# Second mixer: the gate product and the first query product read the input before its norm, and the norm's factor comes in at eviction

## The reference, cut to what matters

```python
x = x + g_f * conv_ffn(...)                # first block: its last product is h @ ffn_w_down
x = rmsnorm(x, final_norm)                 # end of the first block
xn = rmsnorm_2(x, norm_mix_2)              # second block: norm ahead of its mixer
proj = xn @ w_in_2 + b_in_2                # 4608 columns and 16 gate columns
h_q, h_f_fwd, h_f_bwd, h_i, h_g, m_q, ...  = split_cols(proj)
q = silu(h_q)
```

## Time and profile before

| what | value |
|---|---|
| median of 3 runs | 1819.37 us |
| the profiled execution, own time | 1820.89 us |
| its span in the trace | 1819.1 us |
| PE busy | 1725.9 us, 95% |
| DVE busy | 954.3 us, 52% |
| ACT busy | 695.0 us, 38% |
| POOL busy | 148.5 us, 8% |

### The profile page before, as it was taken

One profiled execution on the slowest core, in us unless ns is written; L12 is line 12 of the kernel. 1 busy time (PEld: TensorE's weight loads), 2 busy tenths in 40 slices (PEclk: granted clock), 3 DMA queues, 4 the chain that ended last, 5 costly groups with the idle time before them and its releaser, 6 DMA issues.

```text
span 1819.1 us, 18595 instructions
## 1 busy us (share of the span) xinstructions
PE 1725.9 (95%) x7118; PEld 1276.7 (70%) x7118; DVE 954.3 (52%) x1317; ACT 695.0 (38%) x1016; POOL 148.5 (8%) x158
## 2 busy tenths in 40 slices
PE   7999898989989999999898999989998999999997
PEld 1488644346768888888687877557875778888886
DVE  5867555447444533444639779575534263434343
ACT  2631244311344312333454556874533241313141
POOL 0312200013120000000200000113000100000001
PEclk9999899989999999999899999999998999999999
DMA  9334301330232223222322111334221122233221
GB/s 319 111 115 163 113 10 40 139 116 1 93 91 96 81 74 124 93 75 88 137 103 105 47 47 47 107 122 162 93 93 47 47 93 93 95 110 110 101 92 46
DMA packets 107027, 174.42 MB, mean 96 GB/s; under 512 B 3723, under 2 KB 48267, under 8 KB 106508
## 3 DMA queue, kind: packets, MB, share of 16 engines
q1 hardware_dynamic: 103196, 160.76, 26.0%
q0 software_dynamic: 3760, 12.72, 2.2%
HBM read 169.00 MB, written 4.46 MB: 95 GB/s over the span
## 4 chain that ended last, share of the span: by engine, by line
PE 82%; DVE 7%; ACT 5%; issue 3%; DMA 1%; POOL 1%; SPq 0%; DVEq 0%; ACTq 0%; POOLq 0%
PE bank L822 14%; PE bank L824 14%; PE bank L823 14%; PE bank L855 6%; PE bank L856 6%; PE bank L860 5%; PE bank L876 3%; PE bank L1035 3%; PE bank L1065 2%; PE bank L925 2%; PE bank L1078 1%; PE bank L1005 1%; PE bank L1017 1%; PE bank L1345 1%; PE bank L1376 1%
## 5 line engine op out<-in xcount | busy, mean ns | idle before, releaser
L2916 POOL TENSOR_TENSOR arena<-arena 128x512 f32<-128x512 f32 (+1 forms) x56 | 74.1, 1332 | 986.1 <-ACT arena L1471 982.3
L1440 ACT ACTIVATE weights_hi<-weight_slots 128x2048 fp32r<-128x2048 f32 (+2 forms) x46 | 77.0, 1725 | 123.3 <-DMA weight_slots<-in_ffn_w_down 66.3
L2064 ACT ACTIVATE weights_hi<-weight_slots 128x2048 fp32r<-128x2048 f32 x30 | 55.8, 1908 | 162.0 <-DMA weight_slots<-in_w_up 107.7
L2873 DVE TENSOR_TENSOR weight_slots_lo<-weight_slots,weights_hi 128x2048 fp32r<-128x2048 f32 x30 | 67.4, 2287 | 87.3 <-ACT weights_hi L2064 87.3
L823 PE MATMUL bank<-xn_lo,weights_hi 128*128 128x512 f32 x288 | 112.0, 389 | 0.0
L1426 ACT ACTIVATE arena<-bank 128x512 f32<-128x512 f32 (+3 forms) x110 | 54.7, 537 | 141.9 <-PE bank L824 50.4
L824 PE MATMUL bank<-hx_hi,weight_slots_lo 128*128 128x512 f32 x256 | 99.7, 389 | 0.0
L822 PE MATMUL bank<-sq_hi,weights_hi 128*128 128x512 f32 x256 | 99.6, 389 | 0.0
L823 PE MATMUL bank<-sq_lo,weights_hi 128*128 128x512 f32 x256 | 99.6, 389 | 0.0
L824 PE MATMUL bank<-sq_hi,weight_slots_lo 128*128 128x512 f32 x256 | 99.6, 389 | 0.0
L2114 DVE TENSOR_TENSOR weight_slots_lo<-weight_slots,weights_hi 128x2048 fp32r<-128x2048 f32 (+2 forms) x36 | 70.2, 1990 | 31.1 <-ACT weights_hi L1440 31.1
(11 more groups left out here) (423 smaller groups left out, 4130.5 us busy)
## 6 DMA issues: line engine op xcount, KB each, us to landing
weight_slots<-in_w_in SPq DMA_DIRECT2D x26, 1024.0 KB, 7.1
weight_slots<-in_ffn_w_up SPq DMA_DIRECT2D x22, 1024.0 KB, 7.1
weight_slots<-in_w_mod SPq DMA_DIRECT2D x16, 1024.0 KB, 7.5
weight_slots<-in_w_up SPq DMA_DIRECT2D x16, 1024.0 KB, 6.3
weight_slots<-in_w_down SPq DMA_DIRECT2D x16, 1024.0 KB, 6.2
arena<-in_w_mod POOLq DMA_DIRECT2D x32, 256.0 KB, 3.3
weight_slots<-in_w_out SPq DMA_DIRECT2D x8, 1024.0 KB, 8.5
weight_slots<-in_w_xkv SPq DMA_DIRECT2D x8, 1024.0 KB, 7.5
```

The costliest lines, as they stand in the source:

```text
L1440: A(high_half(kind, n, i), W[:, s_, a:b], ACT.Copy).then_inc(w_hi, 1)
L2064: A(W_hi[:, s % 2, a:b], W[:, s % 2, a:b], ACT.Copy).then_inc(w_hi, 1)
L2873: V.tensor_tensor(W_lo[:, s % 2, a:b], W[:, s % 2, a:b], W_hi[:, s % 2, a:b].bitcast(F32), ALU.subtract).then_inc(w_lo, 1)
L2916: G.tensor_tensor(acc, acc, sq[i % 2][:, 0:width], ALU.add).then_inc(sq_added, 1)
```

## The change

The second mixer's gates and hq are multiplied from xg = x * final_norm * norm_mix_2, without the token factor. ACT writes xg_hi in the loop over the tiles of x, right behind each tile's two squares, by a copy with a scale. DVE writes xg_lo (`gained_low`) inside `half_out`: tile m-1 behind the eviction of product m, for m from 1 on, and tile 7 after the last. DVE then evicts the gates and hq with a multiplication by rstd = r1 * r2, and ACT adds the bias (and takes the silu) in place. PE begins with the high products of tiles 0 and 1, does both norm sums there, and goes on with tiles 2 to 7. hx, normed, is still made for ff, fb and the later slabs. in2 1's high and low parts now stand ahead of hx_hi and hx_lo; x * final_norm * r1 now stands behind the five evictions. in2 1's high parts get a home of their own in the arena, and the product of the gains is formed before the feed-forward stage.

```diff
 PE
-            norm_sum("norm_mid")
-            norm_sum("norm_mix2")
             pe.wait_ge(sem("wgate_lo"), 1)
             w = split_slab("in2", 0)
             ...
             for k in range(KD):
-                pe.wait_ge(x_hi, operand_no["hx", k] + 1)
-                mm(gates[:], wgate_hi[:, k, :], hx_hi[:, k, :], start=k == 0, stop=False)
+                if k == 2:
+                    norm_sum("norm_mid")
+                    norm_sum("norm_mix2")
+                pe.wait_ge(x_hi, operand_no["xg", k] + 1)
+                mm(gates[:], wgate_hi[:, k, :], xg_hi[:, k, :], start=k == 0, stop=False)
 ...
 ACT
                 square_tile("norm_mid", k, x[:, k, :])
                 square_tile("norm_mix2", k, x[:, k, :], scale=pc("final_norm", k))
+                if k == 0:
+                    act.wait_ge(sem("gain_mix2"), 1)
+                A(xg_hi[:, k, :], x[:, k, :], ACT.Copy, scale=gain_mix2[:, k:k + 1]).then_inc(x_hi, 1)
                 if k == KD - 2:
                     split_w("in2", 0)
 ...
+            split_w("in2", 1)
             for k in range(KD):
                 act.wait_ge(normed, norms["norm_mix2"][0] + k + 1)
                 split_x(hx_hi[:, k, :], hx[:, k, :])
-            split_w("in2", 1)
-            ps = full(act, "gates")
-            free(A(zg, ps[:], ACT.Identity, bias=pc("gate_b")), "gates")
+            evicted(act, "gates")
+            A(zg, zg, ACT.Identity, bias=pc("gate_b"))
 ...
 DVE
+            def gained_low(k):
+                dve.wait_ge(x_hi, operand_no["xg", k] + 1)
+                V.scalar_tensor_tensor(xg_lo[k], x[:, k, :], gain_mix2[:, k:k + 1], xg_hi[:, k, :].bitcast(F32),
+                                       ALU.mult, ALU.subtract).then_inc(x_lo, 1)
 ...
                     if half and m == 1:
                         dve.wait_ge(sem("wgate_hi"), 1)
                         V.tensor_tensor(wgate_lo, wgate, wgate_hi.bitcast(F32), ALU.subtract).then_inc(sem("wgate_lo"), 1)
+                    if half and m:
+                        if m == 1:
+                            dve.wait_ge(sem("gain_mix2"), 1)
+                        evicted(dve, f"{kind}_{n - 1}")
+                        gained_low(m - 1)
                     if half and m >= KD - 2:
                         split_w("in2", 0, (m - KD + 2,))
 ...
+            gained_low(KD - 1)
 ...
+            split_w("in2", 1)
             for k in range(KD):
                 split_x("hx", k, hx_lo[:, k, :], hx[:, k, :], hx_hi[:, k, :])
+            for name, dst in [("gates", zg)] + [(f"hq_{m}", q2[:, 512 * m:512 * m + 512]) for m in range(HC)]:
+                ps = full(dve, name)
+                free(V.tensor_tensor(dst, ps[:], rstd[:], ALU.mult), name)
             dve.wait_ge(normed, sum(norms["norm_mix2"]))
             for k in range(KD):
                 V.scalar_tensor_tensor(x[:, k, :], x[:, k, :], pc("final_norm", k), r_mid, ALU.mult, ALU.mult).then_inc(normed, 1)
-            split_w("in2", 1)
```

More of the change, by code:

```diff
@@ L259 @@
 IN2_SPLIT = 6
-HIGH_HOMES = {3: (54, 74), 4: (58, 70), 5: (54, 50)}
+HIGH_HOMES = {1: (32, 40), 3: (54, 74), 4: (58, 70), 5: (54, 50)}
 def split_plan(slab_list):
@@ L271, in operand_plan @@
 def operand_plan():
-    rest = [(n, k) for n in ("hx1", "hc", "mix", "ffn", "hx", "mix2", "mem", "xa", "ao", "mlp") for k in range(KD)]
+    rest = [(n, k) for n in ("hx1", "hc", "mix", "ffn", "xg", "hx", "mix2", "mem", "xa", "ao", "mlp") for k in range(KD)]
     return {k: i for i, k in enumerate(rest)}
@@ L461, in two_blocks @@
         wgate_hi, wgate_lo = (parts("wgate_" + n, a, 2).rearrange("p a c -> p (a c)").rearrange("p (k c) -> p k c", k=KD)
-                              for n, a in (("hi", 42), ("lo", 44)))
+                              for n, a in (("hi", 82), ("lo", 44)))
+        xg_hi = parts("xg_hi", 54, 8)
+        xg_lo = [parts("xg_lo_26", 26, 6)[:, k, :] for k in range(6)] + [parts("xg_lo_14", 14, 2)[:, k, :] for k in range(2)]
         zg, reset = tile(80), tile(81)
@@ L1143, in _ @@
             for k in range(KD):
-                pe.wait_ge(x_hi, operand_no["hx", k] + 1)
-                mm(gates[:], wgate_hi[:, k, :], hx_hi[:, k, :], start=k == 0, stop=False)
-                mm(gates[:], wgate_lo[:, k, :], hx_hi[:, k, :], start=False, stop=False)
+                if k == 2:
[3 more added lines that the diff above has]
+                mm(gates[:], wgate_hi[:, k, :], xg_hi[:, k, :], start=k == 0, stop=False)
+                mm(gates[:], wgate_lo[:, k, :], xg_hi[:, k, :], start=False, stop=False)
                 for c, ps in zip(cols, banks):
-                    mm(ps[:], w[0][:, k, c], hx_hi[:, k, :], start=k == 0, stop=False)
-                    mm(ps[:], w[1][:, k, c], hx_hi[:, k, :], start=False, stop=False)
+                    mm(ps[:], w[0][:, k, c], xg_hi[:, k, :], start=k == 0, stop=False)
+                    mm(ps[:], w[1][:, k, c], xg_hi[:, k, :], start=False, stop=False)
             for k in range(KD):
-                operand("hx", k)
-                ins = mm(gates[:], wgate_hi[:, k, :], hx_lo[:, k, :], start=False, stop=k == KD - 1)
+                operand("xg", k)
+                ins = mm(gates[:], wgate_hi[:, k, :], xg_lo[k], start=False, stop=k == KD - 1)
             end(ins)
@@ L1156, in _ @@
                 for k in range(KD):
-                    ins = mm(ps[:], w[0][:, k, c], hx_lo[:, k, :], start=False, stop=k == KD - 1)
+                    ins = mm(ps[:], w[0][:, k, c], xg_lo[k], start=False, stop=k == KD - 1)
                 end(ins)
             for n, kind in enumerate(["ff", "fb"]):
-                w = split_slab("in2", 1 + n)
+                if n:
+                    w = [(h_, l_) for h_, l_ in zip(*[[v[:, k, :] for k in range(KD)] for v in split_slab("in2", 2)])]
+                else:
+                    pe.wait_ge(w_lo, 2 * split_no["in2", 1] + 2)
+                    lo = low("in2", 1).rearrange("p (k c) -> p k c", k=KD)
+                    w = [(high_parts[1][k // 4][:, k % 4, :], lo[:, k, :]) for k in range(KD)]
                 for m, c in enumerate(cols):
@@ L1163, in _ @@
                     for k in range(KD):
-                        ins = mm3(ps[:], w[0][:, k, c], w[1][:, k, c], hx_hi[:, k, :], hx_lo[:, k, :], k == 0, k == KD - 1)
+                        operand("hx", k)
+                        ins = mm3(ps[:], w[k][0][:, c], w[k][1][:, c], hx_hi[:, k, :], hx_lo[:, k, :], k == 0, k == KD - 1)
                     end(ins)
@@ L1735, in _ @@
                 split_x(hx_hi[:, k, :], hx[:, k, :])
-            split_w("in2", 1)
-            ps = full(act, "gates")
-            free(A(zg, ps[:], ACT.Identity, bias=pc("gate_b")), "gates")
+            evicted(act, "gates")
+            A(zg, zg, ACT.Identity, bias=pc("gate_b"))
             for m in range(HC):
-                ps = full(act, f"hq_{m}")
-                free(A(q2[:, 512 * m:512 * m + 512], ps[:], ACT.Silu, bias=pc("b_in_2", m)), f"hq_{m}")
+                evicted(act, f"hq_{m}")
+                q = q2[:, 512 * m:512 * m + 512]
+                A(q, q, ACT.Silu, bias=pc("b_in_2", m))
             log_exp_tables()
@@ L2405, in _ @@
             link(V.scalar_tensor_tensor(gain_f[:], mod[:, 32:40, 0], 1.0, pc("norm_ffn", 0, 8), ALU.add, ALU.mult))
+            V.tensor_tensor(gain_mix2[:], pc("final_norm", 0, KD), pc("norm_mix_2", 0, KD), ALU.mult).then_inc(sem("gain_mix2"), 1)
             normalise("norm_ffn", lambda k: x[:, k, :], lambda k: gain_f[:, k:k + 1], lambda k: xn[:, k, :])
@@ L2471, in _ @@
                 evicted(dve, f"down_{n}")
-            link(V.tensor_tensor(gain_mix2[:], pc("final_norm", 0, KD), pc("norm_mix_2", 0, KD), ALU.mult))
+            dve.wait_ge(sem("gain_mix2"), 1)
+            gained_low(KD - 1)
             dve.wait_ge(sem("mid_ready"), 1)
```

## The result

| | before | after |
|---|---|---|
| median | 1820.09 us (4 runs, 1817.32 to 1822.19) | 1836.7 us (4 runs, 1835.1 to 1842.17) |
| ratio after to before, 95% interval | | 1.0094 [1.0077, 1.0112] |
| profiled execution, span | 1819.1 us | 1840.4 us (own time 1842.17, the slowest of the four) |
| granted clock, mean | 0.981 | 0.976 |

The change makes the kernel 17 us slower.

A forecast was written before the change was run, and what follows sets the result against it. The prediction took PE's chain as the bound, with time lost where PE waits or runs at half clock. Its terms, 16.1 + 2.6 - 7.7 + 2.6 = +13.6 us, gave a median of 1833.0 us, range 1828 to 1838.

The forecast's parts named there:

- The likeliest case: Whole kernel: all predicted terms come as summed, +13.6 us, median 1833.0 us; chance 54%.
- Term 1: Down products: DVE waits at gained_low(0) for xg_hi 0, holding the cut PE needs for down_12; +16.1 us.
- Term 2: Behind the stall at down_12: PE comes back at half clock; +2.6 us, bounds 1.6 and 3.4.
- Term 3: End of down_15 to ff_0: 34.9 us instead of 42.65, at full clock after a 4.0 us wait; -7.7 us.
- ff_0's cover of hx_lo: Ahead of ff_0: the last hx_lo is ready at 925.3, before ff_0 at 929.4, a cover of 4 us.
- the second rival: Gates' first matmuls and norm sums: the wait for in2 0 drops the clock once more, +2.7 us, 1835.7; chance 18%.
- Term 4: Ahead of fb_0: in2 2's load, issued behind the late store of x, makes PE wait; +2.6 us, bounds 0 and 4.
- The first rival: Ahead of fb_0: in2 2 lands in time or the store is faster, so no wait, 1830.4; chance 20%.
- nothing is added after: Behind the wait at fb_0: ACT and DVE make up their lateness before fb_0 is full; 0 us added.

The follow-up runs named there:

- e1: Changed kernel with the eight xg_lo moved on DVE, behind the evictions of down_13 and down_14 and the cuts of in2 0: 1821.11 us, ratio 1.0014 to before.
- e6: Changed kernel with the high parts of down 5, 6 and 7 taken into ACT's loop over the tiles of x: 1821.38 us, ratio 0.9996 to before.
- e4: Changed kernel with POOL's additions of squares cut to 16 of 512 columns, norm factors no longer the reference's: 1837.49 us, ratio 1.0105 to before.
- e10: Changed kernel with 75 matmuls on idle data ahead of down_12, so PE works through the stall: 1838.65 us, ratio 1.0102 to before.
- e2: Changed kernel with in2 2's load issued ahead of the store of x on SP's queue: 1833.12 us, ratio 1.0073 to before.
- e5: Changed kernel with 68 matmuls on idle data ahead of down_12, the last 2.23 us of the stall left empty: 1838.05 us, ratio 1.0101 to before.
- e9: Changed kernel with e6's and e2's moves, plus in2 0's high parts made and low parts cut earlier: 1808.68 us, ratio 0.9938 to before.
- e11: e9 with 11 matmuls on idle data in the 3.14 us wait ahead of the second projection behind fb_3: 1808.16 us, ratio 0.9934 to before.

## Why the prediction was right, and where its sizes were off

The forecast was 1833.0 us (1828 to 1838) and slower with 0.96; it is 1836.7. The likeliest case came, with more on top of it. That the median stayed inside the range owes something to luck: the terms as the profile has them add up to 21.3 us in place of 13.6, and the profiled execution itself took 1842.17.

- *Term 1, the stall at `gained_low(0)`: predicted +16.1, measured +17.68.* The mechanism is as told: place, releaser, what stands behind it (e1 and e6 take it away by two ways, and the loss goes). xg_lo 0 starts at 860.51, 0.2 us later than predicted. The step that failed is "0.69 us for xg_lo 0, 0.66 us for the eviction and 2.88 us for the two cuts": the cut took 4.37 us, since POOL, set going by the squares at the same moment, adds beside it. 2.88 was read from a stretch in which POOL stood idle. e4 shows it: with POOL's additions cut short 2.91, and a shift of 16.3 us.
- *Term 2, slow clock behind it: predicted +2.6, measured +2.06* in the profile, within the bounds of 1.6 to 3.4. e10 keeps the clock up and gets 1.9 us back there.
- *Term 3, down_15 to ff_0: predicted -7.7, measured -5.61.* The wait ahead of the gates was 3.75 us (4.0 predicted), ff_0's cover of hx_lo held. rstd took 5.5 us (908.37 to 913.83) and not 3.8, which the cover took up. Taking no clock cost was wrong here: the second rival came too, the clock stood at 0.50 until about 904.3, eleven matmuls at 0.43 us. That is 2.5 us by the sum of stretches, against the 2.1 that the term is off. My nearest row, a wait of 3.08 us that left the clock up, was one draw of two: behind that same wait the clock fell in 9 of the 13 profiles and stayed up in 4 (before, after, e2, e5).
- *Term 4, the store ahead of in2 2: predicted +2.6, measured +3.67.* Both were issued at T+6.2 and T+6.6 (T is ff_0's start), the data ended at about T+18.4 (T+17.8 predicted), and the wait is 3.51 us. The first rival (the wait doesn't come) is refuted, and e2 shows that the order on the queue is the cause. Store and load were hardly done faster together than one after the other: from issue to the end of the data the store took 5.5 us alone (902.49 to 908) and the load 7.1 (918.63 to 925.7), both together 12 (938.79 to about 951).
- *Not in the sum: +1.74 between fb_0 and the projection, and +1.8 behind it.* I had set "nothing is added after". The first is the clock, at 0.50 again behind the new wait, by the rows at 960. The second is for the most part the net of the clock's stretches in the rest of the two profiles, 7.5 us lost in after against 6.1 in before: behind the unchanged wait of 3.14 us after lost 3.1 us, before nothing, and before lost more further on.

Of the waits alone (spans less the clock's loss) the difference is 17.7 us. The prediction's own terms without clock are 15.1: 13.6, less 2.6 of term 2, plus the 4.1 us that before lost at its norm sums and gates (1.3 and 2.8 in the sum by stretches), which term 3 had counted as gained. The missing 2.6 us are, to 0.1, what terms 1 and 4 came out larger, 1.6 and 1.1. The profiled run of after is also 5.5 us above its median, so the medians lie 3.7 us above the forecast.

Against the Trainium skill (TensorE: Matmul & The Clock Gate, section "What's actually happening"), the prediction took from its rule that term 2 is a range; the page tells of the matmuls at the start of a kernel, the prediction took it for those behind a pause. The runs agree, with 1.6 to 2.1 us behind the stall in e5, e2 and after, and 3.0 in e4.

## What to carry to other kernels

When an instruction is put into the order of an engine that works in order, look first at what its operand waits for, and then at who is queued behind it: here 0.7 us of new work cost 17.7 us, because its operand stood behind a DMA that landed at 854.78, 17.7 us after DVE had come there (837.08, 23.43 before 860.51), and the cut that PE needed stood behind it. When a helper is set free at the same moment (POOL by the squares), read durations from rows in which it also ran. Compare two profiles from a mark that both share ahead of the change, and not from the start of the span. A good idea that measures slower may only stand in the wrong place: with its three waits mended the change was worth 11 us.

## What the runs showed of the hardware

- DVE and POOL hold each other up. A cut of 128x1280 in two instructions took 2.88 us with POOL idle and 4.37 and 3.99 us beside POOL's additions (after); xg_lo took 0.74 alone and 1.76 to 1.79 beside them (after, e9); POOL's additions took 1.27 us each alone (2.54 for two) and 2.0 to 2.15 beside DVE (8.05 for four, 4.31 for two). The eviction at 861.18, which reads a PSUM bank and one large tile, took 0.75 us beside them as ever. Which side loses depends on which is under way: in e9 POOL's additions begin inside the cut of down 6, the cut still takes 2.88 us, and the additions are long.

  ```profile
  840.78 2.88 DVE L2129 TENSOR_TENSOR weight_slots_lo<-weight_slots,weights_hi 128x1280 fp32r<-128x1280 f32 x2
  842.18 4.32 POOL L2947 TENSOR_TENSOR arena<-arena 128x512 f32<-128x512 f32 x2 [4.13 <-ACT arena L1479]
  ```

  The Trainium skill (SBUF — State Buffer, section "Who interferes with whom") says that a DVE instruction with two SBUF inputs and a GpSimd instruction that reads SBUF block each other; cut, xg_lo and addition are of these kinds, and the rows agree: each took longer beside the other, by up to 1.5 us for the cut, 1.0 for xg_lo and 0.9 for an addition.
- The granted clock after a short wait is no fixed thing. It fell behind a wait of 2.23 us (e5), behind the wait of 3.75 us ahead of the gates in all 7 profiles that have it, behind the one of about 3.5 us ahead of fb_0 in 4 of 6 (not in e4 and e5), behind the same wait of 3.14 us in 7 of 12, and behind that of 3.08 us in 9 of 13. In the stretch of the change (840 to 1020) a fall behind a wait costs 1.3 to 2.1 us where the clock is back after 3 to 4 us of work, and 2.5 to 3.1 where it takes 5 to 6. The loss of whole profiles lies between 18.1 us (e11) and 29.2 (after, e6). The spread among the runs of one kernel goes with it: of the 23 executions of the kernel before in the first batch the fastest, 1816.48 us, has a mean granted clock of 0.985 and the slowest, 1826.88, one of 0.978, and the correlation of time and clock over the 23 is -0.95.
